# A transformer chain in one launch: fifteen more projection units and two output units in split form

## What is computed

```python
def attention_mixer(h, w_in, rel_bias, w_out):
    ...
    proj = h @ w_in
    ...
    return jnp.concatenate([out_a, out_b], axis=-1) @ w_out

def swiglu(h, w_gate, w_up, w_down):
    return (jax.nn.silu(h @ w_gate) * (h @ w_up)) @ w_down
...
    q, f_logit, i, g = jnp.split(u @ w_in, [HGRN_FORGET_DIM, 2 * HGRN_FORGET_DIM,
                                            2 * HGRN_FORGET_DIM + D_MODEL], axis=-1)
    ...
    log_f = jnp.logaddexp(jnp.log(lb), jnp.log1p(-lb) + jax.nn.log_sigmoid(fl))
    k = (1.0 - lb) * jax.nn.sigmoid(-fl)
    q = jax.nn.silu(q.astype(F32))
    ...
    o = rms_norm(o, out_gain) * jax.nn.sigmoid(heads(g.astype(F32), HGRN_VDIM))
    return o.reshape(B, S, D).astype(u.dtype) @ w_out
```

## Time and profile before

| What | us |
|---|---|
| median of 3 runs | 2092.36 (2090.61 to 2092.63) |
| the profiled execution, its own time | 2093.63 |
| span of its trace | 2091.7 |
| TensorE busy | 2065.4 |
| VectorE busy | 1429.7 |
| ScalarE busy | 1210.6 |

### The profile page before, as it was taken

One profiled execution on the slowest core, in us unless ns is written; L12 is line 12 of the kernel. 1 busy time (PEld: TensorE's weight loads), 2 busy tenths in 40 slices (PEclk: granted clock), 3 DMA queues, 4 the chain that ended last, 5 costly groups with the idle time before them and its releaser, 6 DMA issues.

```text
span 2091.7 us, 26804 instructions
## 1 busy us (share of the span) xinstructions
PE 2065.4 (99%) x10550; PEld 1712.9 (82%) x10550; DVE 1429.7 (68%) x1174; ACT 1210.6 (58%) x1117; POOL 79.0 (4%) x142
## 2 busy tenths in 40 slices
PE   9989999999999999999999999999999999999998
PEld 9858889788898668889877888888888888888877
DVE  3755446664436645443646889888888888888797
ACT  3654434653425634333545777786777778777674
POOL 1000000100000000000002100000000000000100
PEclk9999999999999999999999999999999999999999
DMA  8427655566645246645426999999999999999997
GB/s 284 136 86 261 222 184 161 182 212 228 204 149 161 81 141 233 220 161 178 132 85 235 410 368 398 365 394 375 383 378 374 389 363 397 372 389 377 379 402 281
DMA packets 211788, 561.23 MB, mean 268 GB/s; under 512 B 10557, under 2 KB 67998, under 8 KB 211566
## 3 DMA queue, kind: packets, MB, share of 16 engines
q1 hardware_dynamic: 204224, 530.61, 70.1%
q0 software_dynamic: 5552, 28.84, 3.4%
q10 hardware_dynamic: 1934, 0.67, 0.1%
HBM read 553.27 MB, written 16.25 MB: 272 GB/s over the span
## 4 chain that ended last, share of the span: by engine, by line
PE 93%; DVE 3%; ACT 2%; DMA 1%; issue 1%; POOL 0%; DVEq 0%; ACTq 0%; SPq 0%
PE ps L2218 14%; PE ps L2220 14%; PE ps L2219 14%; PE ps L538 9%; PE ps L667 5%; PE ps L669 5%; PE ps L668 5%; PE ps L631 3%; PE ps L708 3%; PE ps L710 3%; PE ps L709 3%; PE ps L570 3%; PE ps L2271 1%; PE ps L694 1%; DMA ring<-in_moe_w_gate 1%
## 5 line engine op out<-in xcount | busy, mean ns | idle before, releaser
L2214 DVE TENSOR_TENSOR ring_r<-ring,ring_r 128x2048 fp32r<-128x2048 f32 x336 | 752.4, 2286 | 103.0 <-ACT ring_r L2209 102.8
L2209 ACT ACTIVATE ring_r<-ring 128x2048 fp32r<-128x2048 f32 x336 | 627.1, 1913 | 68.6 <-DMA ring<-in_moe_w_gate 50.9
L2218 PE MATMUL ps<-ring_r,arena_r 128*128 128x512 f32 x1344 | 530.5, 395 | 1.0 <-DVE arena_r L2472 1.0
L2220 PE MATMUL ps<-ring_r,arena_r 128*128 128x512 f32 x1344 | 524.2, 390 | 0.0
L2219 PE MATMUL ps<-ring_r,arena_r 128*128 128x512 f32 x1344 | 524.0, 390 | 0.0
L340 DVE TENSOR_TENSOR ring_r<-ring,ring_r 128x2048 fp32r<-128x2048 f32 x119 | 272.2, 2291 | 219.4 <-ACT ring_r L331 219.3
L331 ACT ACTIVATE ring_r<-ring 128x2048 fp32r<-128x2048 f32 x119 | 227.4, 1914 | 188.3 <-DMA ring<-in_ffn_w_up 78.2
L2220 PEld LDWEIGHTS ps<-ring_r,arena_r 128*128 128x128 f32 x1344 | 252.6, 188 | 54.0
L2218 PEld LDWEIGHTS ps<-ring_r,arena_r 128*128 128x128 f32 x1344 | 252.8, 188 | 52.4 <-issue 1.2
L2219 PEld LDWEIGHTS ps<-ring_r,arena_r 128*128 128x128 f32 x1344 | 253.0, 188 | 50.7
L667 PE MATMUL ps<-ring_r,arena_r 128*128 128x512 f32 (+1 forms) x576 | 216.0, 375 | 4.7 <-DVE arena_r L452 2.7
(11 more groups left out here) (394 smaller groups left out, 1986.6 us busy)
## 6 DMA issues: line engine op xcount, KB each, us to landing
ring<-in_moe_w_gate SPq DMA_DIRECT2D x115, 1024.0 KB, 5.6
ring<-in_moe_w_up SPq DMA_DIRECT2D x112, 1024.0 KB, 6.2
ring<-in_moe_w_down SPq DMA_DIRECT2D x112, 1024.0 KB, 5.5
ring<-in_ffn_w_gate SPq DMA_DIRECT2D x33, 1024.0 KB, 5.1
ring<-in_ffn_w_up SPq DMA_DIRECT2D x33, 1024.0 KB, 5.1
ring<-in_ffn_w_down SPq DMA_DIRECT2D x33, 1024.0 KB, 5.0
ring<-in_attn_w_in SPq DMA_DIRECT2D x24, 1024.0 KB, 5.7
ring<-in_hgrn_w_in SPq DMA_DIRECT2D x16, 1024.0 KB, 5.5
```

What stands on the lines that cost most here:

```text
L2209: nc.scalar.activation(unit_parts(k)[0], ring[:, slot_of(k), 0:2048], ACT.Copy).then_inc(m_hi, 1)
L2214: nc.vector.tensor_tensor(low, ring[:, slot_of(k), 0:2048], high, ALU.subtract).then_inc(m_lo, 1)
L2218: nc.tensor.matmul(out_, x[:, 0, f, :], w[0], start=first, stop=False)
L2220: return nc.tensor.matmul(out_, x[:, 0, f, :], w[1], start=False, stop=last)
```

## The change

Units that were raw become split: unit 3 of A and its first two output units; units 3 to 7 of E; units 3 to 6, 8 and 12 to 15 of G. The token splits that these need are added in E and G. `first_tokens` takes three units in A, E and G. In E, the first four square roots and reciprocals become a logarithm and an exponential on ACT (`inverse_roots`), and the sums of squares stand two together. In G, sums over time and exponents are interleaved. In F0 and F1, the transposition of t=1 moves into the middle of the unit `up[0, 1]`, and in F0 ACT converts unit `first + 2` earlier. Semaphore counts and pages follow; what is left out below is this bookkeeping.

```diff
@@ -286,8 +284,8 @@
-                         + [(c, "F") for c in (0, 512, 256, 768)] + several("H", 1024, 2), tuple(range(4, 12)))
-        A_out = project_out(a["attn_w_out"][0], (2, 3, 0, 1), raw=2)
+                         + [(c, "F") for c in (0, 512, 256, 768)] + several("H", 1024, 2), tuple(range(3, 12)))
+        A_out = project_out(a["attn_w_out"][0], (2, 3, 0, 1), raw=0)
...
@@ -295,10 +293,10 @@
-        E_plan = project(E_w_in, several("F", 2304, 2) + several("H", 2816, 1) + several("F", 0, 6) + several("H", 1536, 3))
+        E_plan = project(E_w_in, several("F", 2304, 2) + several("H", 2816, 1) + several("F", 0, 6) + several("H", 1536, 3), (3, 4, 5, 6, 7))
-        G_plan = project(G_w_in, several("F", 1024, 4) + several("F", 0, 4) + several("H", 2048, 4) + several("F", 3072, 4))
+        G_plan = project(G_w_in, several("F", 1024, 4) + several("F", 0, 4) + several("H", 2048, 4) + several("F", 3072, 4), (3, 4, 5, 6, 8, 12, 13, 14, 15))
...
@@ -616,13 +614,14 @@
+            skipped = 0 if split_no[plan[0][0]] is not None else 4
-                    xh, xl = (v[:, 2 * (n - 2) + kt, t * P:(t + 1) * P] for v in x_split)
+                    xh, xl = (v[:, 2 * n - skipped + kt, t * P:(t + 1) * P] for v in x_split)
-                        nc.tensor.matmul(o, xh, wh[:, kt, cs], start=False, stop=False)
+                        nc.tensor.matmul(o, xh, wh[:, kt, cs], start=(n == 0 and kt == 0), stop=False)
...
@@ -657,12 +656,12 @@
-            def tokens(u, bank, c, h, t):
+            def tokens(u, bank, c, h, t, part=None):
-                for kt in range(rows_):
+                for kt in range(rows_) if part is None else (2 * part, 2 * part + 1):
...
@@ -720,8 +719,9 @@
-                up_tokens(0, 1, 0)
+                tokens(up[0, 1], 2, 0, 1, 0, 0)
+                tokens(up[0, 1], 2, 0, 1, 0, 1).then_inc(s_u, 1)
...
@@ -948,7 +948,7 @@
-        A_split = [page_r(i)[:, 0:1024].rearrange("p (f t) -> p f t", t=SEQ) for i in (6, 3)]
+        A_split = [page_r(i).rearrange("p (f t) -> p f t", t=SEQ) for i in (6, 4)]
...
@@ -1007,10 +1007,8 @@
-                if m >= 6:
-                    pe.wait_ge(s_ol, split_at["A out"] + m - 6)
-                elif m >= 2:
-                    pe.wait_ge(a_ot, m - 1)
+                if m >= 2:
+                    pe.wait_ge(s_ol, split_at["A out"] + m - 2)
...
@@ -1024,17 +1022,19 @@
-                    pe.wait_ge(*((a_ot, 2 * n + 2) if n < 2 else (s_ol, split_at["A out"] + 2 * n - 3)))
+                    pe.wait_ge(s_ol, split_at["A out"] + 2 * n + 1)
-            first_tokens(pe, 0, first_units(A_plan, 4))
+            first_tokens(pe, 0, first_units(A_plan, 3))
+            pe.wait_ge(s_ol, split_at["A tokens"])
+            half(3, 0)
+            half(3, 1)
+            pe.wait_ge(s_ol, split_at["A tokens"] + 1)
-                if m < 2:
-                    pe.wait_ge(s_ol, split_at["A tokens"] + m)
...
@@ -1069,6 +1069,7 @@
+            highs_to(act, A_plan[3][1])
...
@@ -1113,11 +1114,7 @@
-                if q < 4:
-                    nc.scalar.activation(OT[:, q + 4, :], ps[:, 2 + q % 2, 0:SEQ], ACT.Copy).then_inc(a_ot, 1)
-                else:
-                    act.wait_ge(a_sc, 16)
-                    nc.scalar.activation(A_split[0][:, q - 4, :], ps[:, 2 + q % 2, 0:SEQ], ACT.Copy).then_inc(s_oh, 1)
+                nc.scalar.activation(A_split[0][:, q, :], ps[:, 2 + q % 2, 0:SEQ], ACT.Copy).then_inc(s_oh, 1)
...
@@ -1145,8 +1142,10 @@
+            highs_to(act, A_out[0][0])
+            highs_to(act, A_out[1][0])
...
@@ -1163,11 +1162,12 @@
+            unit_low(3)
+            dve.wait_ge(*used(A_plan[2][1]))
+            nc.vector.tensor_tensor(A_lows[1], HTf, HTh, ALU.subtract).then_inc(s_ol, 1)
-            dve.wait_ge(*used(A_plan[3][1]))
-            nc.vector.tensor_tensor(A_lows[1], HTf, HTh, ALU.subtract).then_inc(s_ol, 1)
...
@@ -1223,6 +1223,11 @@
+            def output_low(q):
+                dve.wait_ge(s_oh, split_at["A out"] + q)
+                nc.vector.tensor_tensor(A_split[1][:, q, :], ps[:, 2 + q % 2, 0:SEQ], A_split[0][:, q, :], ALU.subtract)\
+                    .then_inc(s_ol, 1)
...
@@ -1249,21 +1254,22 @@
+            output_low(0)
+            output_low(1)
+            lows_to(dve, A_out[0][0])
+            output_low(2)
+            output_low(3)
+            lows_to(dve, A_out[1][0])
-            def output_low(q):
-                dve.wait_ge(s_oh, split_at["A out"] + q - 4)
-                nc.vector.tensor_tensor(A_split[1][:, q - 4, :], ps[:, 2 + q % 2, 0:SEQ], A_split[0][:, q - 4, :],
-                                        ALU.subtract).then_inc(s_ol, 1)
...
@@ -1490,7 +1497,7 @@
-        mean_bank = lambda i: 2 if i < 8 else E_banks[10]
+        mean_bank = lambda i: 3 if i in (1, 3) else 2 if i < 8 else E_banks[10]
...
@@ -1498,20 +1505,22 @@
-            first_tokens(pe, 4, first_units(E_plan, 4))
+            first_tokens(pe, 4, first_units(E_plan, 3))
-                unit_tensor(pe, E_plan, j, E_banks, part)
+                unit_tensor(pe, E_plan, j, E_banks, part, E_tokens)
-                elif i:
+                elif i >= 4:
+                elif i >= 2:
+                    pe.wait_ge(e_rt, i - 1)
-                    pe.wait_ge(s_evac, E_plan[2][2] + 1)
+                    pe.wait_ge(s_evac, E_plan[2 + i][2] + 1)
...
@@ -1597,10 +1606,12 @@
-            half(4, 0), sum_squares(0)
-            half(4, 1), sum_squares(1)
-            half(5, 0), sum_squares(2)
-            half(5, 1), sum_squares(3)
+            pe.wait_ge(s_ol, split_at["E tokens"])
+            half(3, None)
+            half(4, 0), sum_squares(0), sum_squares(1)
+            half(4, 1)
+            half(5, 0), sum_squares(2), sum_squares(3)
+            half(5, 1)
...
@@ -1636,6 +1647,10 @@
+            act.wait_ge(s_hth, 4 * 4 + 4)
+            act.wait_ge(s_htl, 4 * 4 + 4)
+            nc.scalar.activation(E_tokens[0], HTf, ACT.Copy).then_inc(s_oh, 1)
+            highs_to(act, E_plan[4][1])
...
@@ -1661,6 +1676,15 @@
+            def inverse_roots(*of):
+                for i in of:
+                    act.wait_ge(e_nn, i + 1)
+                    nc.scalar.activation(E_rs[:, i, :], ps[:, mean_bank(i), :], ACT.Ln, bias=epscol[:, 0:1],
+                                         scale=1.0 / (HD // 2 if i < 2 else HD)).then_inc(e_rt, 1)
+                for i in of:
+                    act.wait_ge(e_rt, i + 1)
+                    nc.scalar.activation(E_rs[:, i, :], E_rs[:, i, :], ACT.Exp, scale=-0.5).then_inc(e_inv, 1)
...
@@ -1689,13 +1713,16 @@
-            for j in range(4):
-                evac(j)
-            root(0), root(1)
+            evac(0), evac(1)
+            highs_to(act, E_plan[5][1])
+            evac(2)
+            highs_to(act, E_plan[6][1])
+            evac(3)
+            inverse_roots(0, 1)
-            root(2)
+            highs_to(act, E_plan[7][1])
+            inverse_roots(2, 3)
-            root(3)
...
@@ -1745,11 +1772,15 @@
+            dve.wait_ge(s_oh, split_at["E tokens"])
+            nc.vector.tensor_tensor(E_tokens[1], HTf, E_tokens[0], ALU.subtract).then_inc(s_ol, 1)
+            lows_to(dve, E_plan[6][1])
-                dve.wait_ge(e_rt, i + 1)
-                nc.vector.reciprocal(E_rs[:, i % 4, :], E_rs[:, i % 4, :]).then_inc(e_inv, 1)
+                if i >= 4:
+                    dve.wait_ge(e_rt, i + 1)
+                    nc.vector.reciprocal(E_rs[:, i % 4, :], E_rs[:, i % 4, :]).then_inc(e_inv, 1)
...
@@ -1801,7 +1832,9 @@
-            normalise(0), normalise(1), normalise(2)
+            normalise(0), normalise(1)
+            lows_to(dve, E_plan[7][1])
+            normalise(2)
...
@@ -1833,7 +1866,7 @@
-        G_q, G_k, G_b, G_g, G_o = (tiles(i) for i in (3, 4, 5, 7, 3))
+        G_q, G_k, G_b, G_g, G_o = (tiles(i) for i in (3, 4, 5, 1, 3))
...
@@ -1860,10 +1894,10 @@
-            first_tokens(pe, 6, first_units(G_plan, 4))
+            first_tokens(pe, 6, first_units(G_plan, 3))
-                unit_tensor(pe, G_plan, j, G_banks, part)
+                unit_tensor(pe, G_plan, j, G_banks, part, G_tokens)
...
@@ -1918,7 +1952,8 @@
-            for j in range(4, 9):
+            pe.wait_ge(s_ol, split_at["G tokens"])
+            for j in range(3, 9):
...
@@ -1941,8 +1976,14 @@
+            act.wait_ge(s_hth, 4 * 6 + 4)
+            act.wait_ge(s_htl, 4 * 6 + 4)
+            nc.scalar.activation(G_tokens[0], HTf, ACT.Copy).then_inc(s_oh, 1)
+            highs_to(act, G_plan[4][1])
+                if u in (1, 2):
+                    highs_to(act, G_plan[u + 4][1])
...
@@ -1959,6 +2000,8 @@
+                if u == 2:
+                    highs_to(act, G_plan[8][1])
...
@@ -2029,10 +2074,15 @@
+            dve.wait_ge(s_oh, split_at["G tokens"])
+            nc.vector.tensor_tensor(G_tokens[1], HTf, G_tokens[0], ALU.subtract).then_inc(s_ol, 1)
+            lows_to(dve, G_plan[4][1])
+                if u in (1, 3):
+                    lows_to(dve, G_plan[5 + u // 2][1])
```

(16 more changed lines are left out.)

18 lines of the change are left out of this document (10 added, 8 removed).

## The result

| | before | after |
|---|---|---|
| median of 4 runs | 2091.49 us (2090.45 to 2092.63) | 2070.12 us (2069.15 to 2071.22) |
| the profiled execution, its own time | 2093.63 | 2071.22 |
| span of its trace | 2091.7 | 2069.7 |

A forecast was written before the change was run, and what follows sets the result against it. PE's own stream was taken to bound the kernel (TensorE busy 2065.4 of 2091.7 us). Gains of 20.3 less 2.5 of new waits gave 17.8 net, so 2074.6 us, range 2070.5 (no new wait and no half clock) to 2079.5.

The forecast's parts named there:

- Price of a unit in each form: On PE: raw half 3.45 us, split half 2.87, or 3.05 alone between raw work; 0.18 per change of form and back.
- A, unit 3: Stage A: unit 3 goes from 7.16 us to 5.74 + 0.18, a gain of 1.2.
- Output blocks: Stage A, output units 0 and 1: four blocks, each between transpositions, gain 0.60 us each, 2.4 in all.
- G: Stage G: units 3 to 6 gain 4.7 us, unit 8 1.0, units 12 and 13 1.6, units 14 and 15 2.0; 9.3 gross.
- F0 and F1: Earlier high half and moved transposition shorten PE's waits: F0 gains 1.7 us (1.1 and 0.6), F1 0.7; bounds nothing and 3.5.
- E's inverse roots and the conversions on DVE: Stage E: DVE gains 13.7 us of lows, loses four reciprocals of 3.35; cost nothing, at most one low, 2.3.
- The waits that come back: New PE waits: E's transposition 0.25 us, A's output low 0.9, G's gate chain 0.6, G's output projection 0.7; together 2.5.
- The late chain: Rival: one more conversion delays G's products or E's scores and PE stands still; about 3 us, 2077.6; chance 0.20.
- The clock at the experts' start: Rival: the half clock there passes if the shift of some 18 us lets it; about 3 us go, 2071.5; chance 0.12.
- Split products at their column count: Rival: new split products start 0.108 us apart instead of 0.12, giving 8.6 us more, 2066; chance 0.01.
- Slower by the half clock in the interleaved stretch: Rival: granted clock falls to 0.50 in E and G; all of E's new halves would make 2110 us; chance 0.02.
- The signs of being wrong: Waits above 3 us before `scores` in E or G, granted clock under 1.00 before the experts, or pitch other than 0.12.

The follow-up runs named there:

- E raw again: The changed kernel with units 3 to 7 of E raw again, everything else as changed: E 147.27 us against 141.45, median 2076.36 us.
- one unit further: The changed kernel with unit 7 of G split too, its conversions standing where unit 8's stood: G 155.34 us against 150.85.
- two variants of the kernel before: The kernel before with only the t=1 transposition moved in F0 and F1 (ratio 0.9991), or only F0's high half made earlier (ratio 0.9996).
- one variant of the kernel before: The kernel before with only the high half of unit first + 2 made earlier in F0: F0 192.37 us against 191.44, ratio 0.9996.
- a kernel that brought this wait in: The changed kernel with A's second output low ahead of the fourth maxima (A 127.47 us against 124.08), or with G's unit 7 split too (G 155.34 against 150.85).

## Why the forecast was right and wrong

The mechanism held: time went out of PE's own stream at the forecast's places, and a few waits came back. The step that failed is the price of a unit in split form, a term that was mis-sized. By its own steps, with the part of the 3.0 us that each stage missed (17.8 forecast, 3.12 + 2.08 + 1.07 + 5.80 + 8.76 = 20.8 by the stages, with F0 at full clock 2.08):

- *Price of a unit in each form.* Here is the fault. The raw half of 3.45 and the split pitch of 0.12 were right, and the isolated split half of 3.05 too. But "each change to the split form and back costs 0.18" was set against raw halves that had no edge cost, because the rows chosen for them, are those in which the next work overlaps. E raw again shows 3.65 for a raw half at the edge, and so does the kernel before, at 660.13. The term must be 0.58 a half, with no edge: that is 15 groups in A, E and G at 0.18, 2.7 us, of which 2.4 shows in the stages. It explains E nearly alone (six groups, 1.08; missed 1.05). That the whole error is 3.0 as well is a balance: the output blocks add 0.3 and the turns 0.6 to 0.7, and the waits take back 0.5 more than forecast.
- *A, unit 3:* 1.2 forecast, about 1.4 measured (from the first transposition to the short products behind unit 3, L887, 31.12 before and 29.72 now). *Output blocks:* 0.60 forecast; PE's rows of one block and its neighbours are 5.04 apart before and 4.36 now, 0.68. The same fault: the block of 3.52 was read from its own start, not from neighbour to neighbour.
- *G:* missed by 0.76. The gate part gave 5.99 instead of 5.7, the four isolated halves 0.39, 0.60, 0.59 and 0.58 instead of 0.40 each (the first has a short stop ahead of unit 12 in it, and its nearness to the forecast's 0.40 is chance), units 14 and 15 about 1.15 each instead of 1.0. Against that the low half of the output projection cost 1.15 instead of 0.7.
- *F0 and F1:* both sources of the wait were right, and 1.1 for the high half was close to the 1.16 estimated above. The turn gives 0.92 and 0.97, not 0.6 and 0.7: taking off for a norm "in the middle" was not needed, since no wait is left there.
- *E's inverse roots and the conversions on DVE:* nothing, as forecast. With E raw again the stage is 147.27, the length before, though the roots are as changed.
- *The waits that come back:* 0.80, 0.52, 0.87 and the 0.25 of E, for 0.9, 0.6, 0.7 and 0.25. This step was the hardest, and its places held. From start to start they cost 0.99, 0.59, 1.15 and 0.25, 3.0 in all and not 2.45.
- *The rivals.* The late chain did not come; one unit further PE stands still for 4.3 us, but for a low half and not for the chain. The clock at the experts' start was "about 3 us" if it passes: in the profiled executions it fell from about 7 us at 0.50 to 3.5, and M is 1.34 shorter. (The prediction says that the clock is low nowhere else; it is 0.50 in the last 2.6 us of the kernel before too, where PE has no work.) But nothing ties this to the shift of 18 us: of two variants of the kernel before, one has 3.4 us there and the other none. Split products at their column count: no, the pitch is 0.12 (G's 192 records from 957.72 take 23.12). Slower by the half clock in the interleaved stretch: E and G ran at 1.00.
- *The signs of being wrong.* One of them came: the granted clock fell under 1.00 before the experts, at F0's start. It does not speak against the sum. A variant of the kernel before has it too, and it costs F0 some 0.6.

The range ended at 2070.5, "no new wait and no half clock". By the prediction's own terms this is 2074.6 less 2.5 of waits less about 3 of clock, 2069.1, so the end was also added up wrong. Without this slip, or with the base of 2091.49 instead of 2092.36 (which moves the end to 2069.6), 2070.12 lies inside; neither says anything of the mechanism, in which the price of a unit stays wrong. The range was built from rivals and waits alone; the price of a unit, from which 15 groups hang, had no bounds of its own, though its two rows (3.45 and 3.05) came from unlike surroundings. With 0 to 0.18 for each group the lower end would have been 2.7 lower, 2067.8.

## To carry to other kernels

Price a replaced piece from neighbour to neighbour, in the surroundings in which it will stand: both forms pay at their edges, and an edge charged to one alone is multiplied by the number of pieces. Each conversion took its own cost out of PE's stream wherever the traces show it, but it brings PE sooner to the next conversion in line, so a gain can end at the first one that comes late, as at unit 12 here. A printed wait can cost more than it says; compare starts. Cut traces at pieces of work that both kernels share; most stages here repeat to a tenth of a microsecond, where medians need microseconds. Look at the clock of each stage before its length.

## What the runs showed of the hardware

**Half-clock stretches go with most of the scatter of one kernel.** Of 34 executions of the kernel before, those with a mean granted clock of 1.000 took 2090.6 (2 of them), with 0.999 on average 2091.2 (17), with 0.998 2092.5 (13), with 0.997 2094.7 (2). The changed kernel has 2069.15 and 2069.50 at 1.000, and 2070.74 to 2072.20 at 0.998 (6). At equal clock the change is worth 21.3 (1.000, two executions each) and 21.2 (0.998). In the traces all of these stretches but two, and but those at the end of the program, stand at two places, behind waits of PE of 0.7 to 1.6 us, and not in every execution: at F0's start in 8 of the 12 traces without idle products there (F0 lasts 0.3 to 0.6 more in the changed kernels; 0.50 for some 7 us made 192.37 of it in one variant of the kernel before), before the experts in 6 of the 11 without idle products there. With them it was 0 of 2 and 0 of 3. At either place this could still be chance, about one in ten by these shares. For the idle products speaks that all 8 executions of the two kernels with idle products at both places had a mean clock of 0.999 or 1.000, against 5 of 12 of the same kernels without them.

The Trainium skill (TensorE: Matmul & The Clock Gate, Part 1) says that the slow state is the default and activity releases it; the drops at the waits of 2.73 in A and 4.26 in G, each in a kernel that brought this wait in, agree.

**A transfer lands 1.5 us later in the kernels with idle products 280 us earlier.** With eight idle products at F0's start F1 lasts 191.9 to 192.1, in both kernels that have them; without, 190.5 to 191.0 in all changed kernels, the one with idle products before the experts alone among them. The transfer is not issued later: SP issues it 3.24 us ahead of F1's first transposition in either case, and it takes 6.4 and 6.6 us in these two kernels, against 4.9 to 5.5 in the others that show it. One thing differs beside it. A transfer of 16 KB in the queue that the profile calls instruction starts 0.5 and 0.8 us behind that transposition in these two, with the weight still under way, and 1.3 to 2.9 us behind it in the others. That the added instructions shift this load into the transfer fits, and no run tests it; what makes the landing late is open.
